# The state-space stage of a two-block kernel: its context part beside the last input pieces, its own PSUM banks for rows and output, and three state buffers

## The reference, cut to what matters

```python
D_MODEL = 1024; SEQ = 512; CTX_LEN = 256; SSD_HEADS = 16; SSD_GROUPS = 4; SSD_STATE = 128

def diff_attend(q, k, v, lam, g_subln, lam_init):
    s = jnp.einsum('bqhcd,bkhcd->bchqk', q, k) * ATTN_SCALE
    p = jax.nn.softmax(s, axis=-1)
    w = p[:, 0] - lam * p[:, 1]
    o = jnp.einsum('bhqk,bkhd->bqhd', w, v)
    ...

def ssd_chunked(xh, dt, a, bm, cm, h0, with_output):
    # h_t = exp(dt_t a) h_{t-1} + dt_t B_t x_t^T,  y_t = C_t h_t
    acum = jnp.cumsum(dtc * a, axis=2)
    to_end = jnp.exp(acum[:, :, -1:] - acum)
    states = jnp.einsum('bcqgn,bcqgr,bcqgrp->bcgrpn', bc, to_end * dtc, xc)
    chunk_decay = jnp.exp(acum[:, :, -1])
    h_last, h_prev = lax.scan(step, h0, (states, chunk_decay))   # h = h * dec + st
    seg = acum[:, :, :, None] - acum[:, :, None]
    decay = jnp.where(lower, jnp.exp(seg), 0.0)
    cb = jnp.einsum('bcign,bcjgn->bcijg', cc, bc)
    y_diag = jnp.einsum('bcijg,bcijgr,bcjgr,bcjgrp->bcigrp', cb, decay, dtc, xc)
    y_off = jnp.einsum('bcign,cbgrpn,bcigr->bcigrp', cc, h_prev, jnp.exp(acum))
    return y_diag + y_off, h_last

# context tokens first (states only), forward and backward; then the latent tokens from those states
y_lat = yf + rev(yb) + d * xh
```

## Time and profile before

| | us |
|---|---|
| median of 3 runs | 3498.79 (3491.78 to 3500.18) |
| the profiled execution, its own time | 3499.95 |
| its span | 3498.1 |

### The profile page before, as it was taken

How to read it: one execution, slowest core, us unless ns; L and a number is a source line. 1 busy time by engine, 2 the same in 40 slices (tenths; PEclk the granted TensorE clock), 3 DMA queues, 4 the chain that set the end, 5 groups by cost and what they waited for, 6 DMA issues and landing times.

```text
span 3498.1 us, 44485 instructions
## 1 busy us (share of the span) xinstructions
PE 3291.1 (94%) x17090; PEld 2591.5 (74%) x17090; DVE 1607.1 (46%) x2268; ACT 1456.2 (42%) x1859; POOL 1304.6 (37%) x1067
## 2 busy tenths in 40 slices
PE   7999997899989999999979999998999998899999
PEld 4787786678746666666557788887888878578887
DVE  4444426555566666666453445545321231452121
ACT  4344434542335555555444555555322242342221
POOL 2222124544303333333325444342444433344444
PEclk9999998999989999999979999999999999999999
DMA  5211110045339999999843222221322212032222
GB/s 209 65 49 59 39 49 13 25 173 179 132 119 340 346 340 344 364 369 359 325 168 114 79 85 91 84 80 67 109 97 97 98 60 73 13 109 97 97 97 73
DMA packets 98532, 496.88 MB, mean 142 GB/s; under 512 B 22446, under 2 KB 22702, under 8 KB 49728
## 3 DMA queue, kind: packets, MB, share of 16 engines
q1 hardware_dynamic: 78480, 454.86, 36.6%
q0 software_dynamic: 19888, 39.73, 3.2%
HBM read 472.48 MB, written 40.89 MB: 147 GB/s over the span
## 4 chain that ended last, share of the span: by engine, by line
PE 80%; DMA 5%; DVE 5%; ACT 4%; issue 4%; POOL 1%; SPq 0%; POOLq 0%; ACTq 0%; DVEq 0%
PE ps L283 13%; PE ps L285 13%; PE ps L284 13%; PE ps L1963 7%; DMA arena<-we_gu 4%; PE ps L289 4%; PE ps L291 3%; PE ps L290 3%; PE ps L1948 2%; PE ps L1952 2%; PE ps L1951 2%; PE ps L2501 1%; PE ps L2489 1%; PE ps L677 1%; PE ps L2471 1%
## 5 line engine op out<-in xcount | busy, mean ns | idle before, releaser
L283 PE MATMUL ps<-arena_r,arena_r 128*128 128x512 f32 x2080 | 826.0, 397 | 22.2 <-POOL ring_r L273 6.6
L284 PE MATMUL ps<-arena_r,arena_r 128*128 128x512 f32 x2080 | 814.6, 392 | 0.0
L273 POOL TENSOR_TENSOR ring_r<-ring,arena_r 128x512 fp32r<-128x512 f32 x400 | 550.8, 1408 | 659.4 <-ACT arena_r L268 659.4
L268 ACT ACTIVATE arena_r<-ring 128x2048 fp32r<-128x2048 f32 x166 | 316.6, 1908 | 407.7 <-PE ps L285 331.4
L283 PEld LDWEIGHTS ps<-arena_r,arena_r 128*128 128x128 f32 x2080 | 393.4, 189 | 113.9 <-issue 22.9
L273 POOL TENSOR_TENSOR arena_r<-ring,arena_r 128x512 fp32r<-128x512 f32 x264 | 335.2, 1302 | 381.0 <-ACT arena_r L268 381.0
L284 PEld LDWEIGHTS ps<-arena_r,arena_r 128*128 128x128 f32 x2080 | 393.9, 189 | 81.6 <-issue 1.9
L285 PE MATMUL ps<-arena_r,arena_r 128*128 128x512 f32 x1056 | 410.8, 389 | 0.0
L285 PE MATMUL ps<-arena_r,ring_r 128*128 128x512 f32 x1024 | 403.6, 394 | 0.0
L2051 DVE TENSOR_TENSOR arena_r<-arena,arena_r 128x2048 fp32r<-128x2048 f32 x132 | 301.8, 2288 | 171.9 <-ACT arena_r L2009 171.9
L2009 ACT ACTIVATE arena_r<-arena 128x2048 fp32r<-128x2048 f32 x132 | 250.7, 1910 | 131.6 <-DMA arena<-we_gu 108.8
(11 more groups left out here) (436 smaller groups left out, 5811.3 us busy)
## 6 DMA issues: line engine op xcount, KB each, us to landing
ring<-wstream SPq DMA_DIRECT2D x177, 1024.0 KB, 4.9
arena<-we_gu SPq DMA_DIRECT2D x132, 1024.0 KB, 8.2
arena<-we_down SPq DMA_DIRECT2D x66, 1024.0 KB, 7.6
arena<-arena SPq DMA_DIRECT2D x256, 64.0 KB, 2.0
arena<-ys SPq DMA_DIRECT2D x32, 512.0 KB, 6.9
arena<-wstream SPq DMA_DIRECT2D x24, 512.0 KB, 7.1
arena<-x_t SPq DMA_DIRECT2D x2, 2048.0 KB, 13.0
rope<-wstream SPq DMA_DIRECT2D x8, 512.0 KB, 8.5
```

Of the source, the lines that this page charges most:

```text
L268: act.activation(whalf(c, 0), ring[:, c % NSLOT, :], ACT.Copy).then_inc(sem("chunk_hi"), 1)
L273: ins = pool.tensor_tensor(whalf(c, 1)[:, q:q + 512], ring[:, c % NSLOT, q:q + 512], whalf(c, 0)[:, q:q + 512].bitcast(F32), ALU.subtract)
L283: pe.matmul(out, hi, rhs[0], start=start, stop=False)
L284: pe.matmul(out, hi, rhs[1], start=False, stop=False)
```

## The change

Eight edits, most of them in the scan.

1. `chunk_hi` leaves `evacuate` and becomes `next_high`, called after `turned` in the attention loop.
2. The context's transposes, ACT copies and DVE scalings move among the last granules: the first tile after granule 21 of 24, the second after granule 22. They get buffers of their own (`CXW` four, `CBTOK` two). `dt_sums_scalar` moves one granule ahead.
3. The sums: `dt_tensor` writes them twice, in partitions 0 to 63 and 64 to 127; the upper copy becomes the low half. One matmul now adds both, so `rows` has 2 matmuls, not 4.
4. Rebuilding the tokens and the skip term move from DVE to POOL; the skip term becomes one 128x4096 multiplication.
5. Rows always in banks 4 and 5, output always in banks 6 and 7.
6. The decays' exponential is written **in place in SBUF** (`DM`), and DVE's multiplication reads both of its inputs from SBUF.
7. `XDT` and `CBM` twice; three state buffers that rotate, so that POOL writes the decayed state into a free one and DVE adds in place.
8. New orders on all engines: PE puts the next `turn` behind the first half of the output; DVE's order in a step is add state, mask (q=1), scale next tokens, differences, add output, mask inner, mask (next, q=0).

```diff
-            if closes_chunk(g) and c + 2 < CH_XBC + 8:
-                chunk_hi(act, c + 2)
+        def next_high(act, g):
+            c = place(g)[0]
+            if closes_chunk(g) and c + 2 < CH_XBC + 8:
+                chunk_hi(act, c + 2)
...
                 evacuate(act, 8 + n)
                 if n < NU:
                     turned(act, n)
+                next_high(act, 8 + n)
...
+                if g == QKV_GRANULES + 21:
+                    context_turn(pe, 0)
+                if g == QKV_GRANULES + 22:
+                    context_turn(pe, 1)
...
             for x in range(NU + 2 - XBC_AT - 1, 24):
+                if x in (21, 22):
+                    context_weighted(dve, x - 21)
                 taps(dve, x)
...
+        def rebuild_gpsimd(pool):
+            products_done(pool, QKV_GRANULES + 22)
+            for k in range(KT):
+                ins = XX.rebuild(pool, k)
+            ins.then_inc(sem("xbc_rebuilt"), 1)
+            pool.wait_ge(sem("xbc_rebuilt"), 1)
+            pool.wait_ge(sem("xbc_silu"), 4)
+            pool.tensor_tensor(Y, XBC[:, 0:KT, TC:TA], v("d_skip").unsqueeze(2).to_broadcast([P, KT, T]),
+                               ALU.mult).then_inc(sem("ssd_skip"), 1)
...
+                for half in range(2):
+                    mm = pe.matmul(SUM_ROWS[64 * half:64 * half + 64, d * P:d * P + P],
+                                   DTA[:, d, 2:AT, :].rearrange("p a b -> p (a b)"), TRI[d], start=True, stop=True)
...
+        XDT = [view(W1 + 4096, 1024), view(R + 30720, 1024)]
+        CBM = [view(W1 + 6656, SSD_G, P), view(R + 32256, SSD_G, P)]
+        STATE = [view(R, 1024), view(R + 1024, 1024), view(R + 32768, 1024)]
...
             def rows(m, q):
+                if m or q:
+                    pe.wait_ge(sem("ssd_erow"), 2 * m + q)
                 for i in range(2):
                     at = 1024 * q + 512 * i
-                    for part in range(2):
-                        mm = pe.matmul(bank(half_bank(m, q) + i), PICK_STEP[:, pick * P:pick * P + P],
-                                       ROW_BLOCKS[part][:, at:at + 512], start=(part == 0), stop=(part == 1))
+                    mm = pe.matmul(bank(4 + i), PICK_TILE[:, (t - 2) * P:(t - 1) * P], ROW_BLOCKS[d][:, at:at + 512],
+                                   start=True, stop=True)
...
             for m in range(len(STEPS)):
                 output(m, 0)
+                turn_step(m + 1)
+                rows(m + 1, 0)
                 output(m, 1)
+                inner(m + 2)
+                rows(m + 1, 1)
+                state(m + 1)
...
+            def masked(m, q):
+                dve.wait_ge(sem("ssd_cb"), m + 1)
+                dve.wait_ge(sem("ssd_exp"), 2 * m + q + 1)
+                dm = DM[:, 8 * q:8 * q + 8, :].rearrange("p (g r) i -> p g r i", r=4)
+                dve.tensor_tensor(dm, dm, CBM[m % 2][:, 2 * q:2 * q + 2, :].unsqueeze(2).to_broadcast([P, 2, 4, P]),
+                                  ALU.mult).then_inc(sem("ssd_decay"), 1)
...
+            copy_state(0)
+            scaled_tokens(0)
+            mask_inner(0)
+            differences(0)
+            copy_state(1)
+            mask_inner(1)
+            masked(0, 0)
+            for m in range(len(STEPS)):
+                add_state(m)
+                masked(m, 1)
+                scaled_tokens(m + 1)
+                differences(m + 1)
+                add_output(m)
+                mask_inner(m + 2)
+                masked(m + 1, 0)
...
+                act.activation(EC[:, 8 * q:8 * q + 8, :].rearrange("p h i -> p (h i)"), bank(4, 1024),
+                               ACT.Exp).then_inc(sem("ssd_erow"), 1)
+                dm = DM[:, 8 * q:8 * q + 8, :].rearrange("p h i -> p (h i)")
+                act.activation(dm, dm, ACT.Exp, scale=(1.0, -1.0)[q]).then_inc(sem("ssd_exp"), 1)
...
+            for m in range(len(STEPS)):      # ACT
+                keys(m + 1)
+                exponents(m + 1, 0)
+                exponents(m + 1, 1)
...
+            rebuild_gpsimd(pool)
+            weighted(0)
+            row_terms(0, 0)
+            decayed(0)
+            for m in range(len(STEPS)):
+                row_terms(m, 1)
+                weighted(m + 1)
+                decayed(m + 1)
+                row_terms(m + 1, 0)
```

More of the change, by code:

```diff
@@ L616, in qkv_scalar @@
                 evacuate(act, g)
+                next_high(act, g)
         def qkv_gpsimd(pool):
@@ L1010, in two_blocks, with state_buffers @@
         NSTATE = len(STEPS) - 2
-        SCALED = view(R + 32768, 1024)
-        WCOL = view(S0 + 960, 2, 2, SSD_H)
[L1013 to L1018, removed]
+        def state_buffers():
+            now, spare, old, new = [0, 1], 2, [], []
+            for m, (d, t) in enumerate(STEPS):
+                old.append(now[d])
+                new.append(spare)
+                if m < NSTATE:
+                    now[d], spare = spare, now[d]
+            return old, new
@@ new lines, in two_blocks, with turn @@
+        OLD, NEW = state_buffers()
+        WCOL = view(S0 + 960, 2, 2, SSD_H)
+        CXW = [[view(W1 + 2048 + 1024 * d, 1024) for d in range(2)], [view(R + 32768 + 1024 * d, 1024) for d in range(2)]]
+        CBTOK = (BTOK, view(R + 30720, 512))
+        def turn(pe, i, t, with_b):
+            tok = slice(t * P, t * P + P)
+            for j in range(KT):
+                mm = pe.transpose(bank(0, P, j * P), XBC[:, j, tok], C["ident"])
+            mm.then_inc(sem("ssd_xturn"), 1)
+            if with_b:
+                for g in range(SSD_G):
+                    mm = pe.transpose(bank(2, P, g * P), XBC[:, 8 + g, tok], C["ident"])
+                mm.then_inc(sem("ssd_bturn"), 1)
@@ new lines, in context_turn, with context_keys, context_weights @@
+        def context_turn(pe, t):
+            if t:
+                pe.wait_ge(sem("ssd_cxw"), 2)
+                pe.wait_ge(sem("ssd_btok"), 1)
+            else:
+                pe.wait_ge(sem("xbc_silu"), 6)
+            turn(pe, t, t, True)
+        def context_keys(act, t):
+            act.wait_ge(sem("ssd_bturn"), t + 1)
+            act.activation(CBTOK[t], bank(2), ACT.Copy).then_inc(sem("ssd_btok"), 1)
+        def context_weights(dve):
+            link = Link(dve, "dve_link")
+            dve.wait_ge(sem("dt_ends"), 2)
+            link(dve.tensor_tensor(WCOL, DT[:, :, 0:2, :], TOEND[:, :, 0:2, :], ALU.mult))
+            for d in range(2):
+                ins = dve.tensor_tensor(WCOL[:, d, d, :], WCOL[:, d, d, :], DECAY[:, d, 1 - d, :], ALU.mult)
+            link(ins)
@@ L1048, in rows, with turn_step @@
                 mm.then_inc(sem("ssd_rows"), 1)
[L1050 to L1058, removed]
+            def turn_step(m):
+                if m >= len(STEPS):
+                    return
+                if m:
+                    pe.wait_ge(sem("ssd_xdt"), m)
+                    pe.wait_ge(sem("ssd_state"), min(m, NSTATE))
+                else:
+                    pe.wait_ge(sem("ssd_cxw"), 4)
+                pe.wait_ge(sem("ssd_btok"), min(m + 2, NSTATE + 2))
+                turn(pe, m + 2, STEPS[m][1], m < NSTATE)
@@ L1090, in state @@
                 mm.then_inc(sem("ssd_statemm"), 1)
[L1092 removed]
             for t in range(2):
[L1094 to L1112 removed]
+                context_state(t, 0)
@@ L1113, in ssd_tensor @@
+            turn_step(0)
+            inner(0)
+            rows(0, 0)
+            for t in range(2):
+                context_state(t, 1)
+            inner(1)
+            rows(0, 1)
+            state(0)
+            for m in range(len(STEPS)):
                 output(m, 0)
-                if m + 1 < len(STEPS):
-                    rows(m + 1, 0)
+                turn_step(m + 1)
+                rows(m + 1, 0)
                 output(m, 1)
-                if m < NSTATE:
-                    state(m)
```

304 lines of the change are left out of this document (148 added, 156 removed).

## The result

The changed kernel takes 3467.02 us (median of 4, 3459.89 to 3471.0) against 3499.48 us (median of 4): 0.9904 of before, 95% interval 0.9887 to 0.9922. The forecast was 3470 us, 29.2 us gained; the medians differ by 32.5. The profiled execution took 3471.0 us, with a span of 3469.1, which is 29.0 less than the span before. In a second series, on another chip with the kernel before beside it, the same kernel stood at 0.9912 (0.9899 to 0.9925).

What follows compares the result with a forecast made beforehand. PE at work bounds 80% of the span, so gains lie where PE waits, in the attention loop and the scan. 15.0 + 14.9 - 0.7 = 29.2 us off the 3498.79 median gives 3470 us, own range 3465 to 3476.

Steps and rivals of the forecast that it cites:

- turned copy first: Attention loop, chunk ends: PE's 11 waits for ACT's turned copy go, 15.0 us gained; 9 if another wait is next.
- head: POOL's weighted tokens start: Ahead of the scan: after rebuild and skip term, POOL's queue reaches the weighted tokens at 546.8 us, the others ready 546.9.
- head: gain up to differences 1: Ahead of the scan: differences of step 1 start at 558.6 instead of 573.45, 14.9 us gained, range 12.5 to 17.
- mask q=1, from ready to end: Scan step: DVE's mask, ready 1.05 us after POOL's row terms start, waits for their 2.37 us, then takes 1.0.
- a step: Scan: a step takes 12.0 us against 11.88, 10.8 without DVE and POOL taking turns; range 10.8 to 14.4.
- six steps, gain: Scan: six steps cost 72.0 us against 71.3, so 0.7 us is lost.
- end of the scan, gain: From the last step's differences to the phase end: 15.8 us after, 15.9 before, nothing changes.
- The overlap of 0.24 us: Scan step: alternating DVE and POOL operations overlap by 0.24 us each, so the 1.22 us mask adds 1.0 after POOL's.
- Rival D: Scan: PE's share falls to 76%, its clock drops to 1.2 GHz, a step has 18.2 us of PE: 3511; chance 0.05.

Runs made afterwards that it cites:

- products in PSUM: Changed kernel with masked inner products kept in a PSUM bank, inner products made one step ahead instead of two: 3453.83 us, 0.9893 of the kernel before.
- order alone: Changed kernel with inner products made one step ahead instead of two, mask still with two SBUF inputs: 3465.02 us, 0.992 of the kernel before.
- POOL's operation in halves: Changed kernel with each of POOL's row-term operations (128x1024) cut into two of 128x512: 3467.91 us, 0.9917 of the kernel before.
- both edits: Changed kernel with masked inner products in PSUM and the skip term on ACT: 3453.31 us, 0.9874 of the kernel before.
- the repeat: Changed kernel, nothing altered, measured again in the second series beside the kernel before: 3466.81 us, 0.9912 of the kernel before.

## Why the prediction was right

By its own steps, in us:

| step | forecast | measured |
|---|---|---|
| turned copy first | 15.0 | 14.6, alone 14.5 |
| head: POOL's weighted tokens start (15.9 of the loop taken off) | 546.8 - 15.9 = 530.9 | 530.86 |
| head: gain up to differences 1 | 14.9 | 15.2 |
| mask q=1, from ready to end | 2.4 | 2.40 as recorded, 2.58 from ACT's end |
| a step | 12.0 | 11.82, the last 12.66 |
| six steps, gain | -0.7 | -0.5 |
| end of the scan, gain | 0 | -0.1 |
| sum | 29.2 | 29.1 by these steps (from unrounded times), 29.0 by the span, 32.5 by the medians |

- **The attention loop.** Right, term and cause. The wait list gave the price nearly whole, as the plain iteration beside it showed no next wait; 0.4 of the 15.0 did not come, beside 1.0 us of new small waits for ACT.
- **The head.** The sum is right, and small errors in its terms cancel, which is luck in the last half microsecond. The context was hidden as forecast. I followed POOL's queue, which the trace after shows unbroken. The rebuild started 0.4 us later than forecast (513.82 against 529.3 - 15.9 = 513.4), and the skip term took 7.02 us, not 7.6. One detail went another way: the first mask came 0.2 us before POOL's row terms (532.52), not after them, so POOL waited (3.33 us for 2.37) and not DVE; the sum is the same. Of the pieces of this gain only the skip term was run alone; the hidden context and the moved rebuild are read from the trace and not shown by a run of their own.
- **The step.** The three chained gains of the change (own banks, free buffers, rows by one matmul) are real together: 11.88 to 10.56 with the mask out of POOL's way. Which of them gives how much, no run separates. The second SBUF input takes 1.26 of these 1.32 us back. This was the step against which the change's own effect had to be weighed, and rows 12 and 13, two lines of another phase, carried it. Three runs move it as expected: mask in SBUF alone +1.35 a step, products in PSUM -1.26, order alone 0. With POOL's operation in halves it is -0.16, in the expected direction, with masks of 1.4 and 1.9, but less than the 0.3 to 0.6 expected. That the six steps came out at -0.5 for -0.7 is partly luck: five of them were 0.18 shorter than 12.0 each (0.9 together), and the last was 0.66 longer, for the clock.
- **The overlap of 0.24 us** that I took from the row instead of a full wait: masks end 1.07 us after POOL's operation, for 1.22 alone, so the overlap is 0.15: there, as the row said, but smaller. That makes the step 0.1 longer than forecast; it came out at 11.82 all the same, since two other terms were each 0.14 too long: from the differences to POOL's row terms it is 7.31 us for 7.45, and behind the mask the scaled tokens take 1.06 for 1.2. By the rule of the Trainium skill ("SBUF — State Buffer", Who interferes with whom), without overlap, the step would have been 12.2; the trace agrees with the rule in kind, and the measurement is 0.4 below it, of which the overlap is 0.15 and the rest is these two terms.
- **Rival D**, the clock, is the one piece of truth that the forecast left at nothing. It does not fall in the steps at PE's share of 79% (46.75 of 59.12), but it fell twice behind them, for the outputs of step 6, at a cost of 0.8 us, and for those of step 7, at none, in both traces of the changed kernel. The place was the end, where the state matmuls are gone and PE's pause reaches 2.8 us. All three other kernels with long masks in the new order lost it at the outputs of step 6 as well (order alone, halves, skip term on ACT; pauses of 2.8 to 2.9 us). Before, a pause of 2.45 us left the clock whole:

```profile
652.56 0.45 PE L1080 MATMUL ps<-arena 128*64 128x128 f32 x4 [2.45 <-DVE arena L1171]
```

  At the outputs of step 6 the pause is 1.75 us both with the products in PSUM, where the clock stayed whole, and with both edits, where it fell. So the pause alone does not decide it; what does is left open.
- **The end of the scan.** The prediction's terms add up to 15.7 us, not to its 15.8, and 15.96 was measured, against 15.88 before. POOL's low half took 5.51 us for 4.94, as it waited for the last mask (622.73 to 625.21) for 0.6 us and not 0.4.
- **The difference of medians**, 32.5 against 29.2, is not traced to a step. In the traces the phase with the change ends 30.5 us earlier, 1.3 us of it from before the attention loop, and the repeat's medians differ by 31. The interval of the ratio (27 to 40 us) holds all of these.

## What to carry to other kernels

Before an operand moves from PSUM to SBUF, look at what POOL does at that moment: in these traces a DVE operation with two SBUF inputs waits for the POOL operation that runs, and POOL's next then waits for it (masks of 1.22 us take 2.40 to 3.00, a POOL operation of 1.91 takes 2.88). Here one such operand took back nearly all that double buffers and free banks gave in the loop, and putting the other operand into PSUM gave it again. When the same operation has two lengths in a trace, subtract its ends from those of the neighbour engine: the wait is hidden in its busy time and in no wait list.

A copy that another engine waits for goes ahead of one that nobody waits for yet. Here that is the moving of one call, and by the traces half of the whole gain (14.6 of 29.1 us).

## What the runs showed of the hardware

- A DVE operation on 128x64 elements took 3.38 us (504.30, above), as it met a POOL operation of 3.6 us; the two on 128x16 behind it took 3.58 together, beside POOL's second one. Before, with POOL idle, they took 0.21 and 0.26. Small operations with two SBUF inputs paid the same turn as large ones. Here it was just off the path: DVE's scalings behind them ended at 513.68, and the second context transposes, which need them, began at 513.74, straight behind PE's last product.
- POOL pays too: 2.69, 2.88 and 3.33 us for operations of 2.38, 1.91 and 2.37.
- On POOL one multiplication by a value broadcast along the innermost dimension costs 1.91 us for 1024 columns and 7.02 for 4096, one whose inputs both run along it (row terms, rebuild) 2.37 for 1024 and 1.25 for 512 (9.97 for eight).
